# Moving one of eight tiles of a depthwise convolution from VectorE to GpSimd, and slowing VectorE's pace of taps

## The reference, cut to what matters

```python
q, k, v, glu_a, glu_b, gate_sb, gate_cv = jnp.split(proj, offs, axis=-1)
o_sb = stick_breaking_attention(q, k, v)            # 8 heads of 128
o_sb = o_sb @ w_sb_out
u = glu_a * jax.nn.sigmoid(glu_b)                   # 256 tokens x 1024 channels
u = causal_depthwise_conv(u, w_dw, b_dw)            # 31 taps, each channel by itself
u = jax.nn.silu(layernorm(u, g_conv_ln, b_conv_ln))
o_cv = u @ w_conv_out
merged = sigmoid(gate_sb) * o_sb + sigmoid(gate_cv) * o_cv
```

## Time and profile before

| what | value |
|---|---|
| median of three runs | 3088.13 us |
| the profiled execution: own time | 3087.87 us |
| its span (first to last instruction) | 3086.2 us |
| TensorE busy, share of the span | 3073.5 us, 100% |
| VectorE busy | 2050.1 us, 66% |
| ScalarE busy | 1585.0 us, 51% |
| GpSimd busy | 738.9 us, 24% |
| granted TensorE clock, all 40 slices | 9 (90% or more of full speed) |

### The profile page before, as it was taken

How to read it: one execution, slowest core, us unless ns; L and a number is a source line. 1 busy time by engine, 2 the same in 40 slices (tenths; PEclk the granted TensorE clock), 3 DMA queues, 4 the chain that set the end, 5 groups by cost and what they waited for, 6 DMA issues and landing times.

```text
span 3086.2 us, 43287 instructions
## 1 busy us (share of the span) xinstructions
PE 3073.5 (100%) x16769; PEld 2651.0 (86%) x16769; DVE 2050.1 (66%) x2938; ACT 1585.0 (51%) x2259; POOL 738.9 (24%) x567
## 2 busy tenths in 40 slices
PE   9999999999999999999999999999999999999999
PEld 7888888888888888888888888888888888888887
DVE  8957985555555655555555689998766846555554
ACT  7654454444444444444444656666566544444454
POOL 0023368888740201111110300000431000100013
PEclk9999999999999999999999999999999999999999
DMA  7567878999876877777776555555555555556564
GB/s 253 171 205 268 312 189 192 215 215 214 215 214 212 280 229 228 243 249 246 249 221 191 187 185 171 178 174 188 190 189 175 190 188 189 191 191 190 188 190 136
DMA packets 328573, 640.25 MB, mean 207 GB/s; under 512 B 56752, under 2 KB 216752, under 8 KB 325296
## 3 DMA queue, kind: packets, MB, share of 16 engines
q1 hardware_dynamic: 256560, 573.91, 59.0%
q10 hardware_dynamic: 34944, 63.42, 5.8%
q0 software_dynamic: 36864, 0.15, 3.2%
HBM read 605.80 MB, written 31.59 MB: 207 GB/s over the span
## 4 chain that ended last, share of the span: by engine, by line
PE 95%; DVE 3%; ACT 1%; issue 0%; DMA 0%; POOL 0%; SPq 0%; POOLq 0%; ACTq 0%; DVEq 0%
PE G L489 47%; PE G L493 24%; PE G L544 4%; PE M L542 4%; PE M L544 4%; PE G L543 4%; PE G L542 4%; PE M L543 4%; DVE lo L1138 1%; DVE CV L1486 1%; ACT hi L795 0%; DVE tS L1148 0%; PE M L619 0%; PE M L605 0%; DVE tS L1144 0%
## 5 line engine op out<-in xcount | busy, mean ns | idle before, releaser
L489 PE MATMUL G<-ZA,hi 128*128 128x512 f32 x5104 | 1767.4, 395 | 3.3 <-DVE lo L1138 2.2
L1138 DVE TENSOR_TENSOR lo<-raw,hi 128x1024 fp32r<-128x1024 f32 x1088 | 1362.7, 1271 | 472.0 <-ACT hi L795 471.2
L493 PE MATMUL G<-ZA,lo 128*128 128x256 f32 x5120 | 1389.4, 277 | 0.0
L795 ACT ACTIVATE hi<-raw 128x1024 fp32r<-128x1024 f32 x1088 | 1119.2, 1053 | 414.2 <-DMA raw<-in_pv 363.2
L489 PEld LDWEIGHTS G<-ZA,hi 128*128 128x128 f32 x5104 | 943.8, 188 | 209.9 <-DVE lo L1138 2.7
L493 PEld LDWEIGHTS G<-ZA,lo 128*128 128x128 f32 x5120 | 962.1, 188 | 17.4
L802 ACT ACTIVATE tA<-G 128x256 f32<-128x256 f32 x430 | 163.5, 381 | 750.0 <-PE G L493 749.8
L489 PE MATMUL G<-ZB,hi 128*128 128x512 f32 x1520 | 526.0, 394 | 0.0
L1773 POOL DMA_INDIRECT g_scratch<-sel,IDX x256 | 406.7, 1589 | 115.1 <-issue 83.7
L493 PE MATMUL G<-ZB,lo 128*128 128x256 f32 x1536 | 422.4, 277 | 0.0
L1144 DVE TENSOR_TENSOR tS<-G,tA 128x256 f32<-128x256 f32 x336 | 141.1, 420 | 333.5 <-ACT tA L802 332.0
(11 more groups left out here) (322 smaller groups left out, 1984.3 us busy)
## 6 DMA issues: line engine op xcount, KB each, us to landing
raw<-in_pu SPq DMA_DIRECT2D x256, 512.0 KB
raw<-in_pv SPq DMA_DIRECT2D x256, 512.0 KB
raw<-in_w_in SPq DMA_DIRECT2D x192, 512.0 KB
raw<-in_w_up SPq DMA_DIRECT2D x128, 512.0 KB
raw<-in_w_down SPq DMA_DIRECT2D x128, 512.0 KB
raw<-in_w_out SPq DMA_DIRECT2D x32, 512.0 KB
raw<-in_wq SPq DMA_DIRECT2D x32, 512.0 KB
g_scratch<-zero ACTq DMA_DIRECT2D x16, 1024.0 KB, 6.5
```

The costliest lines, as they stand in the source:

```text
L489: pe.matmul(G[:, 0:512], w, Z[:, k, :], start=first, stop=False, skip_group_check=True)
L493: m = pe.matmul(G[:, 0:256], lo[POS[u][p] % NRAW][:, k % 8, :], weights(u, p)[1][:, k, 0:256], start=False, stop=last, skip_group_check=True)
L795: act.activation(hi[w][:, :, :], raw[r][:, :].rearrange("p (k n) -> p k n", k=8), ACT.Copy).then_inc(s_hi, 1)
L1138: dve.tensor_tensor(lo[r][:, :, :], raw[r][:, :].rearrange("p (k n) -> p k n", k=8), hi[w][:, :, :].bitcast(F32), ALU.subtract).then_inc(s ...
```

## The change

The eighth tile of the convolution goes to GpSimd, which has no instruction here that multiplies by a column and adds a tensor in one: each tap is a product into a scratch tile `tQ` (the weight's column spread over 256 elements) and a sum into the tile's place in `CV`, 62 instructions in all. GpSimd issues them at its step 351, before its sums for the layer norm. VectorE keeps seven tiles, 217 taps where there were 248, and its pace is now three taps on steps with an attention job and four on the others up to step 363, then five. ScalarE's wait before it overwrites the `UC` buffers, and GpSimd's own sum of the eighth tile, wait for a second semaphore `s_dwp`.

```diff
-TAPS_FIVE = range(SG + 4, SG + 9)
+DVE_TILES = 7
@@ ScalarE
-                        act.wait_ge(s_dw, 8 * TAPS)
+                        act.wait_ge(s_dw, DVE_TILES * TAPS)
+                        act.wait_ge(s_dwp, 2 * TAPS)
@@ VectorE
-                for x in range(first, min(first + count, 8 * TAPS)):
+                for x in range(first, min(first + count, DVE_TILES * TAPS)):
@@ VectorE
-                    n = min(4 if AT0[0] <= u < SG + 12 and u not in TAPS_FIVE else 5, TAPS * DW_READY[u] - taps)
+                    pace = (3 if attention_at(u, AT_DVE) else 4) if AT0[0] <= u < SG + 12 else 5
+                    n = min(pace, TAPS * min(DVE_TILES, DW_READY[u]) - taps)
@@ GpSimd
+            def depthwise():
+                j = DVE_TILES
+                b, out = UC[j % 5], CV[:, j, :]
+                pool.wait_ge(s_glu, j + 1)
+                pool.wait_ge(s_mean, 4)
+                for k in range(TAPS):
+                    t = tQ[k % 2]
+                    pool.tensor_tensor(t[:, :], b[:, k:k + 256], C("w_dw", 8 * k + j).broadcast_to([128, 256]), ALU.mult).then_inc(s_dwp, 1)
+                    if k:
+                        pool.wait_ge(s_dwp, 2 * k)
+                    pool.wait_ge(s_dwp, 2 * k + 1)
+                    pool.tensor_tensor(out, C("b_dw", j).broadcast_to([128, 256]) if k == 0 else out, t[:, :], ALU.add).then_inc(s_dwp, 1)
@@ GpSimd
+                if u == SG - 1:
+                    depthwise()
                 for j in SUM_AT.get(u, ()):
-                    pool.wait_ge(s_dw, TAPS * (j + 1))
+                    if j < DVE_TILES:
+                        pool.wait_ge(s_dw, TAPS * (j + 1))
+                    else:
+                        pool.wait_ge(s_dwp, 2 * TAPS)
```

More of the change, by code:

```diff
@@ L339, in build @@
             sem(n) for n in ("s_xg", "s_nfp", "s_nfd", "s_rc", "s_xs"))
-        s_ucp, s_sgl, s_glu, s_dw, s_qkv, s_vtm, s_vt, s_qk, s_zt, s_spx, s_spm1, s_trm, s_tri, s_ex, s_avm, s_av = (
-            sem(n) for n in ("s_ucp", "s_sgl", "s_glu", "s_dw", "s_qkv", "s_vtm", "s_vt", "s_qk", "s_zt", "s_spx", "s_spm1", "s_trm", "s_tri", "s_ex", "s_avm", "s_av"))
+        s_ucp, s_sgl, s_glu, s_dw, s_dwp, s_qkv, s_vtm, s_vt, s_qk, s_zt, s_spx, s_spm1, s_trm, s_tri, s_ex, s_avm, s_av = (
+            sem(n) for n in ("s_ucp", "s_sgl", "s_glu", "s_dw", "s_dwp", "s_qkv", "s_vtm", "s_vt", "s_qk", "s_zt", "s_spx", "s_spm1", "s_trm", "s_tri", "s_ex", "s_avm", "s_av"))
         s_sig, s_lns, s_lnu, s_lnc, s_lnq, s_lnt, s_lnx, s_sgm, s_sil = (
```

## The result

The changed kernel takes 3093.14 us (median of 22 runs, 3091.91 to 3097.55) where the kernel before takes 3088.20 in as many: a ratio of 1.0015, 95% interval 1.0010 to 1.0021. It is slower by 4.9 us, 0.15%. Predicted were +2.8 us and 3090.9 us. The profiled execution took 3093.79 us, 0.65 above the median, for a span of 3092.0 us, which is 5.8 us longer than before.

The account below looks back on a forecast made before the run. TensorE was taken as the bound, nearly always busy, with VectorE nearly full behind it. Removing the first wait (-0.8) and adding the M1 stall (+3.6) gave +2.8 us, 3090.9 us; 8-in-10 range 3087.2 to 3097.0 us.

Parts of the forecast that it names:

- The first wait goes: TensorE's wait for the first pair's exponential near 1881 us disappears, since VectorE has three taps fewer by then: -0.8 us.
- GpSimd's work: GpSimd's 62 instructions from 1978 us, nearly all stretched to 0.9 to 1.7 us, end near 2040; their length costs nothing.
- products as long as sums: Sign on GpSimd that the forecast is wrong; it took 0.61 us for a product, 0.74 for a sum.
- the rival of the dear product: GpSimd's product costs VectorE what a sum does: M1 stall 5.7 us, 3093.8 us; 30 in 100 above +6.2 us.
- Collisions: VectorE instructions reading two SBUF tensors are delayed beside GpSimd, 10.3 us in all before unit 353's scaling.
- The stall at M1: TensorE waits before the last pair's first scores, VectorE's scaling being 8.4 us late: +3.6 us.
- The clock: Rival: TensorE falls to 1.2 GHz during the M1 stall, 2.8 us more, 3093.7 us; 5 in 100.
- The last pair's exponential adds nothing: VectorE is 8.0 us late there against 5.4 us of room, but TensorE has already moved by 3.6: no added time.
- the splits have 8.6 us of room: VectorE's split weights have 8.6 us before TensorE needs them, so no wait is added.
- VectorE absorbs it: Rival: fewer than 15 collisions before unit 353's scaling, no stall at M1, 3087.3 us; 12 in 100.

Follow-up runs that it names:

- pace undone: Changed kernel with VectorE's old numbers of taps per step, the tile staying on GpSimd; 3099.98 us, ratio 1.0040.
- one kind only, products: Changed kernel with GpSimd doing the 31 products and one sum, 30 sums left out; 3091.66 us, one execution.
- one kind only, sums: Changed kernel with GpSimd doing one product and the 31 sums, other products left out; 3093.30 us, one execution.
- four filling matmuls: Changed kernel with four unneeded matmuls on TensorE ahead of the last pair's wait for bank M1; 3092.28 us, ratio 1.0015.
- early copy: Changed kernel with ScalarE's copy out of M1 moved ahead of its evacuation of unit 353; 3092.92 us, ratio 1.0017.
- GpSimd slower: Changed kernel with GpSimd issuing its taps one or two to a step, from step 350 to 370; 3096.63 us, ratio 1.0031.
- ten unread copies: Kernel before, with ten copies that nobody reads on ScalarE ahead of its copy out of M1; 3095.23 us, ratio 1.0023.
- eight unread copies: Kernel before, with eight copies that nobody reads on ScalarE ahead of its copy out of M1; 3092.97 us, ratio 1.0013.

## Why the prediction was right, and where it was not

*The first wait goes, -0.8 us.* Right: 1.02 us by TensorE's start times, and partly back when the pace was undone.

*GpSimd's work: 62 instructions, stretched, ending near 2040; products cheaper than sums.* Right, though the sign that was named for it, shorter products, does not show in the means. Its groups from 1970 to 2110, product and sum of a tap (busy us, mean ns):

```profile
L1790 POOL TENSOR_TENSOR tQ<-UC,col 128x256 f32<-128x256 f32 x31 | 31.3, 1009 | 199.0 <-DVE UC L1228 199.0
L1794 POOL TENSOR_TENSOR CV<-CV,tQ 128x256 f32<-128x256 f32 x30 | 29.5, 983 | 4.3
```

The last ends at 2041.98. In company both take about 1 us, waits behind VectorE included, and "products as long as sums" was a sign of being wrong: these means alone would have spoken for the rival of the dear product, and so would the time, 3093.1 us against its 3093.8. The shortest say otherwise: 0.61 us for a product, as was taken, and 0.72 for a sum of two tiles. That rival also had a stall of 5.7 us where 3.4 came. What a product costs VectorE, 0.10 us less per tap, is seen in the two runs with one kind (0.13 was taken). By the rule of the Trainium skill ("GPSIMD Engine Reference", section 3.1) that a two-input instruction there is held by its read port, the product would last as long as the sum; the shortest of each, 0.61 and 0.72 us, are against it here.

*Collisions: 0.36 us a tap, 0.54 a split, 0.15 a scaling, 0.13 less for half of them, nothing for the join.* Right in all that weighs. VectorE's groups from 1978 to 2046, beside GpSimd, and from 2050 to 2066, without it:

```profile
L1139 DVE TENSOR_TENSOR lo<-raw,hi 128x1024 fp32r<-128x1024 f32 x19 | 31.2, 1678 | 0.0
L1487 DVE SCALAR_TENSOR_TENSOR CV<-UC,col,CV 128x256 f32<-128x256 f32 x33 | 26.6, 807 | 0.8
L1149 DVE TENSOR_TENSOR tS<-tS,R 128x256 f32<-128x256 f32 x9 | 4.2, 468 | 0.3
L1145 DVE TENSOR_TENSOR tS<-G,tA 128x256 f32<-128x256 f32 x9 | 3.7, 411 | 0.0
...
L1139 DVE TENSOR_TENSOR lo<-raw,hi 128x1024 fp32r<-128x1024 f32 x8 | 9.4, 1218 | 0.0
L1487 DVE SCALAR_TENSOR_TENSOR CV<-UC,col,CV 128x256 f32<-128x256 f32 x11 | 5.3, 483 | 0.3
L1149 DVE TENSOR_TENSOR tS<-tS,R 128x256 f32<-128x256 f32 x3 | 1.3, 424 | 0.1
L1145 DVE TENSOR_TENSOR tS<-G,tA 128x256 f32<-128x256 f32 x3 | 1.2, 417 | 0.0
```

A tap costs 0.32 us more, a split 0.46, a scaling 0.04, the join nothing; with the cheaper products taken off, the prediction had about 0.30, 0.48 and 0.09. VectorE's scaling of unit 353 was 7.64 us late by the clock of the trace. Against TensorE, which until the stall ran 0.59 us ahead of the kernel before (its transposes at 2008.91, before that as below), these are 8.2 us. Forecast were 8.4.

```profile
2009.50 0.60 PE L632 MATMUL M<-con,qkv 128*128 128x128 f32 x4
```

*The stall at M1, 8.4 - 3.96 - 0.8 = 3.6 us.* Right: 3.39 us in the view of waits, 3.56 by TensorE's start times. With the first wait that makes +2.5 us; the sum was +2.8.

*The clock.* This step failed. The forecast left TensorE at full speed behind the stall and gave the fall of the clock 5 in 100, as a rival, at 2.8 us; it cost 2.85 us in the profiled execution, and -0.8 + 3.6 + 2.8 was that rival's 3093.7 us. For this alone the measured +4.9 us lies outside the +0.5 to +4.5 that the forecast had for itself, in the stretch up to +6.2 that it had given to the dear product. The trace of before had no wait near 3.6 us; that was no evidence for a low chance. The Trainium skill ("TensorE: Matmul & The Clock Gate", Part 1) says that an idle TensorE falls to half its clock: the trace agrees with its 0.50, and the run with a wait of 2.9 us and a clock of 1.00 shows that it doesn't follow from every wait.

*The last pair's exponential adds nothing; the splits have 8.6 us of room.* Right in the result, wrong in the working. ScalarE and TensorE there, the answer to the earlier trace rows:

```profile
2066.55 0.85 ACT L998 ACTIVATE zs<-zs 128x768 f32<-128x768 f32 x1
```

```profile
2068.87 0.59 PE L658 MATMUL M<-zs,VT 128*128 128x256 f32 x2
```

1.5 us of room were left. But the exponential came 9.73 us later than before (at 2066.55 for 2056.82), and VectorE's third job ahead of it as much, where 8.0 were forecast. VectorE from its scaling of unit 353 to that job, before and after (columns as above):

```profile
2003.76:2053.16 49.40, 49.40 (x290) 43.42 (x289) 43.97 (x72) 28.60 (x40) 0.84 (x1) 1.00 0.53 171
2011.40:2062.89 51.49, 49.98 (x274) 43.70 (x275) 50.49 (x64) 28.29 (x39) 33.13 (x34) 0.93 0.48 153
```

Its idle time fell from 5.4 to 1.0 us, and its taps by eight, both as counted. What was short is the company: 34 instructions of GpSimd met it there, 30 of the tile and four sums that stand behind the tile in GpSimd's queue. The forecast counted 26 and gave the sums no price; at its 0.31 us each, 34 are 10.5 us and not 8.1, and 7.64 + 10.5 - 4.4 - 3.9 makes 9.8. This did no harm by luck: the fall of the clock, which the forecast had left out as well, held TensorE back by 2.85 us more, and the room was 1.5. With the stall or the slow matmuls taken away the room is gone: 1.1 us of wait in the run with four filling matmuls, 2.1 + 2.1 us with the early copy. So some 4 us of the loss could not be had back at M1 at all, only on VectorE.

*VectorE absorbs it.* It did not with the taps as the change deals them out; it does with two a step beside GpSimd.

## What to carry to other kernels

Work that was moved to GpSimd was paid for by VectorE instruction by instruction, wherever VectorE's read two tensors from SBUF: here about 0.3 us for each of GpSimd's 62, an estimate of 19 us for a tile that takes 16 us off VectorE. What VectorE is spared has to lie in the same steps in which GpSimd works, not before and behind them. Count GpSimd's other instructions that the move puts beside VectorE as well. Count the next place behind each stall with TensorE where it would be without the stall, since a wait that is taken away hands the lateness on to the next one. And where a stall of some us is forecast for TensorE, put a fall of its clock beside it as an even chance, with its own price: in the table below it came behind seven of eleven waits of 1.9 us and more.

## What the runs showed of the hardware that was not expected

How TensorE's granted clock answers to a single wait. The cost is what TensorE's matmuls lose after the wait, by their start times:

| kernel | wait, us | granted clock behind it | cost, us |
|---|---|---|---|
| one kind only, products | 1.9 | 0.83 from 2010 to 2020 | 1.7 |
| GpSimd slower | 2.0 | 0.81 from 2121 to 2130 | 1.6 |
| pace undone, last pair | 2.7 | 0.94 from 2050 to 2110 | 3.0 |
| changed kernel | 3.4 | 0.50 from 2012.0 to 2018.7 | 2.8 |
| pace undone, M1 | 4.3 | 0.96 from 2010 to 2050 | 1.5 |
| ten unread copies | 4.7 | 0.50 from 2014.4 to 2019 | 2.3 |
| one kind only, sums | 4.8 | 0.83 from 2010 to 2020 | 1.7 |
| GpSimd slower, last pair | 1.9 | 1.00 | 0.1 |
| early copy, split and last pair | 2.1, 2.1 | 1.00 | 0.1, 0.1 |
| eight unread copies | 2.9 | 1.00 | 0.1 |

A clock over a longer stretch is its mean. The wait's length alone does not decide: the clock fell after one of 1.9 us and not after one of 2.9. Each of the four waits above 3 us brought a fall, those of 1.1 us (four filling matmuls) and 1.3 us (GpSimd slower) did not, and the price did not grow with the wait. The 22 times of the changed kernel spread over 3091.9 to 3094.2 us but for one, those of the kernel before over 3087.4 to 3090.2; whether different falls of the clock make that spread was not shown, since only one execution of each kernel is profiled. What decides between 1.9 and 2.9 us stays open.
